# First norm of a two-layer diffusion trunk: modulation columns on TensorE in four groups, token squares summed in PSUM, first FFN pair chunk by chunk

## What is computed

```python
mod = (silu(c) @ ada_w[i] + ada_b[i])          # 9 * 1024 columns; c for latents, c_ctx for context
h   = x * rsqrt(mean(x * x) + eps) * g * (1 + mod[1]) + mod[0]
x   = x + 0.5 * mod[2] * ((silu(h @ w_gate) * (h @ w_up)) @ w_out)
```

## Time and profile before

| what | value |
|---|---|
| median of 3 runs | 2604.01 us (2602.99 to 2610.74) |
| the profiled execution | 2606.32 us, its span 2604.5 us |
| busy PE / DVE / ACT / POOL | 96% / 61% / 34% / 17% of the span |
| first 130 us, moved by DMA | 21.57 MB, 166 GB/s |
| first FFN matmul of the core | 77.26 us after the span's start |
| loop of FFN pairs (L1225) begins | 97.82 us |

### The profile page before, as it was taken

One profiled execution on the slowest core, in us unless ns is written; L12 is line 12 of the kernel. 1 busy time (PEld: TensorE's weight loads), 2 busy tenths in 40 slices (PEclk: granted clock), 3 DMA queues, 4 the chain that ended last, 5 costly groups with the idle time before them and its releaser, 6 DMA issues.

```text
span 2604.5 us, 40617 instructions
## 1 busy us (share of the span) xinstructions
PE 2510.9 (96%) x14679; PEld 2223.4 (85%) x14679; DVE 1598.4 (61%) x2500; ACT 874.5 (34%) x1358; POOL 436.7 (17%) x524
## 2 busy tenths in 40 slices
PE   6999999999799999999999999999899988999999
PEld 6888888888788888888889999998889977788887
DVE  6788667224678867883484756574777774433332
ACT  1333223122533322332242433243456553322221
POOL 2022111001212211110100000001477751000000
PEclk6899999999899999999999999999899999899999
DMA  6355543221145544542111222122110101233332
GB/s 222 109 149 157 145 126 105 64 75 39 33 133 150 168 129 129 149 145 67 44 57 57 81 59 79 50 80 65 49 49 24 48 25 57 73 100 94 93 102 87
DMA packets 363902, 238.77 MB, mean 92 GB/s; under 512 B 7633, under 2 KB 362546, under 8 KB 363826
## 3 DMA queue, kind: packets, MB, share of 16 engines
q1 hardware_dynamic: 361984, 237.01, 31.2%
q10 hardware_dynamic: 1842, 0.77, 0.1%
HBM read 235.65 MB, written 2.10 MB: 91 GB/s over the span
## 4 chain that ended last, share of the span: by engine, by line
PE 89%; DVE 5%; issue 2%; ACT 2%; POOL 1%; DMA 0%; SPq 0%; ACTq 0%; DVEq 0%; POOLq 0%
PE pu L1225 62%; PE pu L1373 11%; PE pv L1511 5%; PE pu L1233 3%; PE pu L1548 1%; DVE h_lo L2070 1%; PE pv L1539 1%; PE pu L1529 1%; DVE xn L2062 1%; POOL sqa L632 1%; PE pv L1301 1%; PE pu L1484 1%; DVE mx L2169 1%; PE pu L1635 1%; DVE a L2188 0%
## 5 line engine op out<-in xcount | busy, mean ns | idle before, releaser
L1225 PE MATMUL pu<-h_hi,w_hi 128*128 128x512 f32 x1776 | 506.9, 350 | 1.9 <-DVE w_lo L1757 1.8
L1225 PE MATMUL pu<-h_lo,w_hi 128*128 128x512 f32 x1776 | 506.2, 349 | 0.0
L1225 PE MATMUL pu<-h_hi,w_lo 128*128 128x512 f32 x1776 | 504.9, 348 | 0.0
L1757 DVE TENSOR_TENSOR w_lo<-w_raw,w_hi 128x1024 fp32r<-128x1024 f32 (+3 forms) x228 | 310.5, 1362 | 242.6 <-ACT w_hi L755 234.6
L755 ACT ACTIVATE w_hi<-w_raw 128x1024 fp32r<-128x1024 f32 (+3 forms) x228 | 247.8, 1088 | 574.1 <-PE pu L1225 510.0
L1774 DVE SCALAR_TENSOR_TENSOR ada_acc<-ada_raw,cs,ada_acc 128x384 f32<-128x384 f32 x588 | 337.3, 615 | 10.7 <-DVE ada_acc L1774 1.8
L1225 PEld LDWEIGHTS pu<-h_hi,w_hi 128*128 128x128 f32 x1776 | 284.1, 188 | 48.6 <-DVE w_lo L1757 2.2
L1225 PEld LDWEIGHTS pu<-h_hi,w_lo 128*128 128x128 f32 x1776 | 285.3, 188 | 46.3
L1225 PEld LDWEIGHTS pu<-h_lo,w_hi 128*128 128x128 f32 x1776 | 284.0, 188 | 44.1
L1985 DVE SCALAR_TENSOR_TENSOR xT<-pu,gate,xT 128x512 f32 (+3 forms) x136 | 81.3, 633 | 332.2 <-PE pu L1225 329.1
L684 POOL TENSOR_TENSOR ada_acc<-ada_acc,ada_parts 128x768 f32<-128x768 f32 x84 | 142.3, 1694 | 707.3 <-ACT ada_parts L762 667.0
(11 more groups left out here) (266 smaller groups left out, 4540.2 us busy)
## 6 DMA issues: line engine op xcount, KB each, us to landing
w_raw<-in_ffn_w_in SPq DMA_DIRECT2D x138, 512.0 KB, 3.9
ada_raw<-in_ada_w SPq DMA_DIRECT2D x84, 768.0 KB, 4.7
w_raw<-in_ffn_w_out SPq DMA_DIRECT2D x48, 704.0 KB, 4.6
w_raw<-in_ffn_w_in SPq DMA_DIRECT2D x76, 256.0 KB, 3.0
w_raw<-in_diff_w_qkv SPq DMA_DIRECT2D x24, 512.0 KB, 5.4
first_h<-in_ada_w SPq DMA_DIRECT2D x4, 1536.0 KB, 20.1
w_raw<-in_ffn_w_out SPq DMA_DIRECT2D x16, 384.0 KB, 3.5
w_raw<-in_ffn_w_out SPq DMA_DIRECT2D x16, 320.0 KB, 3.1
```

Of the source, the lines that this page charges most:

```text
L1225: last = pe.matmul(banks(ch, s_), w[:, j, :], r[:, SEG[s_]], start=(j == 0 and i == 0), stop=(j == k - 1 and i == 2))
L1757: dve.tensor_tensor(w_lo[:, ch, 0:k * P], w_raw[:, ch, 0:k * P], w_hi[:, ch, 0:k * P].bitcast(F32), ALU.subtract).then_inc(split_ready[ch], 1)
```

## The change

It rewrites the setup up to the end of the first FFN pair, in five parts.

1. All shift and scale columns are multiplied on PE. They are loaded and multiplied in four groups of two chunks of shift and two of scale (32 products each). DVE's shares and PE's sums over them are gone. The two gate chunks that were in the setup are loaded and multiplied after FFN pair 1.
2. PE sums each chunk's squares right away, with six products by the column of ones per chunk, added up in PSUM, between the transposes. POOL's additions are gone.
3. DVE runs the norm group by group, two chunks of both sections, as soon as that group's columns are there.
4. PE's first FFN pair goes chunk by chunk, with both sections and both channels for each chunk, and the column products of groups 2 and 3 stand between the chunks.
5. SP loads group 0, the first pair's weights and group 1, waits for the last transpose (groups 2 and 3 lie over the token stage), and then loads those.

```diff
-            for u in range(ADA_FIRST):
-                sp.dma_start(first_raw[u], first[:, :, u, :]).then_inc(first_in[u], 16)
+            def load_first(g):
+                for m in range(2):
+                    sp.dma_start(first_raw[:, g, :, m, :], first[:, :, m, 2 * g * P:2 * (g + 1) * P]).then_inc(first_in[g], 16)
...
+            load_first(0)
+            for ch in range(2):
+                load_unit(ch, 0, wslot(w_raw, ch, DC), ...)
+            load_first(1)
+            sp.wait_ge(xt_done, DC)
+            load_first(2)
+            load_first(3)
             load_ffn(0)
...
-            sum_chunks(0)
+            for s_ in range(2):
+                inv_rms_tokens(0, s_)
...
+            for j in range(DC):
+                act.wait_ge(x_ready, j + 1)
+                if j >= 2:
+                    act.wait_ge(x_sums, j - 1)
+                act.activation(sq[:, j % 2, :], xT[:, j, :], ACT.Square).then_inc(sq_ready, 1)
             for ch in range(2):
                 split_hi(ch, 0, DC)
-            norm_act(0)
+            for j in range(DC):
+                for s_ in range(2):
+                    norm_hi(0, s_, j)
...
+                            first_pair()
+                            for ch in range(2):
+                                unit(ch, 1, DC, lambda j: h_hi[:, j], lambda j: h_lo[:, j], n)
+                            gate_products()
+                            first = 2
...
+            def first_products(g, cols=(0, 1)):
+                pe.wait_ge(first_in[g], 32)
+                for c_ in cols:
+                    for m in range(2):
+                        at = first_at(g, m) + 2 * c_
+                        for j in range(DC):
+                            last = pe.matmul(pv[:, 2 + g % 2, at:at + 2], first_raw[:, g, j, m, c_ * P:(c_ + 1) * P],
+                                             cs[:, j::DC], start=(j == 0), stop=(j == DC - 1))
+                last.then_inc(first_done, 1)
...
+            def token_sums(j):
+                pe.wait_ge(sq_ready, j + 1)
+                own = j == DC - 1
+                for s_ in range(2):
+                    for t in range(*tiles(0, s_)):
+                        at = TT * own + t
+                        last = pe.matmul(sum_cols(s_)[:, at:at + 1], sq[:, j % 2, t * P:(t + 1) * P], ones[:, 0:1], ...)
...
+            def first_pair():
+                for ch in range(2):
+                    pe.wait_ge(split_ready[ch], 2)
+                for g in range(GROUPS):
+                    for j in (2 * g, 2 * g + 1):
+                        for s_ in range(2):
+                            pe.wait_ge(h_ready[s_], j + 1)
+                        for ch in range(2):
+                            last = chunk(ch, j, DC, h_hi[:, j], h_lo[:, j], NT)
+                            if j == DC - 1:
+                                last.then_inc(unit_done[ch], 1)
+                    if g + 2 < GROUPS:
+                        first_products(g + 2)
...
+                if j >= 2:
+                    token_sums(j - 2)
...
+            first_products(0, (0,))
+            token_sums(DC - 2)
+            token_sums(DC - 1)
+            first_products(0, (1,))
             for s_ in range(2):
                 spread(0, s_)
-            first_sums(2)
-            first_sums(3)
+            first_products(1)
             ffn_pe(0)
...
-            first_share(0)
-            first_share(1)
-            first_share(2)
             for s_ in range(2):
                 norm_rms(0, s_)
-            first_share(3)
...
+            for g in range(GROUPS):
+                first_mods(g)
+                if g == 0:
+                    for ch in range(2):
+                        split_lo(ch, 0, DC)
+                for j in (2 * g, 2 * g + 1):
+                    for s_ in range(2):
+                        norm_scale(0, s_, j)
+                for j in (2 * g, 2 * g + 1):
+                    for s_ in range(2):
+                        norm_lo(0, s_, j)
```

More of the change, by code:

```diff
@@ L548, in load_ffn @@
                     if q == 0 and ADA_COUNT[n]:
-                        for f in range(2):
+                        for f in range(int(n == 0), 2):
                             in_pair(0, f, False)
                         sp.wait_ge(h_ready[1], DC * (2 * n + 1))
+                        if n == 0:
+                            sp.dma_start(gate_raw[:], first[:, :, 2, 0:GATE_CH * P]).then_inc(gate_in, 16)
                         load_granule(n, 0)
@@ new lines, in gate_products @@
+            def gate_products():
+                pe.wait_ge(gate_in, 16)
+                for c_ in range(GATE_CH):
+                    at = 2 * (GATE_FIRST + c_)
+                    for j in range(DC):
+                        pe.matmul(pv[:, 2, at:at + 2], gate_raw[:, j, c_ * P:(c_ + 1) * P], cs[:, j::DC],
+                                  start=(j == 0), stop=(j == DC - 1))
+            def token_sums(j):
[4 more added lines that the diff above has]
+                        at = TT * own + t
+                        last = pe.matmul(sum_cols(s_)[:, at:at + 1], sq[:, j % 2, t * P:(t + 1) * P], ones[:, 0:1],
+                                         start=(j == 0 and t == tiles(0, s_)[0] or own), stop=(j >= DC - 2), skip_group_check=True)
+                    if own:
+                        last.then_inc(var_done, 1)
+                if not own:
+                    last.then_inc(x_sums, 1)
@@ L2066, in norm_seg @@
                     if j + 1 < DC:
[L2067 to L2071, removed]
+                        norm_scale(i, s_, j + 1)
+                    norm_lo(i, s_, j)
                     if j in at:
@@ L2073, in norm_seg, with first_mods @@
                         at[j]()
+            def first_mods(g):
+                dve.wait_ge(first_done, g + 2)
+                for m in range(2):
+                    c0, at = DC * m + 2 * g, first_at(g, m)
+                    last = dve.tensor_tensor(mod[:, :, c0:c0 + 2], pv[:, 2 + g % 2, at:at + 4].rearrange("p (c s) -> p s c", s=2),
+                                             par[:, 0:1, c0:c0 + 2].broadcast_to((P, 2, 2)), ALU.add)
+                last.then_inc(first_mod, 1)
+                dve.wait_ge(first_mod, 2 * g + 1)
+                c0 = C_NORM_G + 2 * g
+                dve.scalar_tensor_tensor(amul[:, 0, :, 2 * g:2 * g + 2], mod[:, :, DC + 2 * g:DC + 2 * g + 2], 1.0,
+                                         par[:, 0:1, c0:c0 + 2].broadcast_to((P, 2, 2)), ALU.add, ALU.mult).then_inc(first_mod, 1)
+                dve.wait_ge(first_mod, 2 * g + 2)
```

131 lines of the change are left out of this document (49 added, 82 removed).

## The result

| | before | changed |
|---|---|---|
| median | 2604.86 us (4 runs, 2602.99 to 2610.74) | 2630.11 us (4 runs, 2627.85 to 2634.44) |
| ratio | | 1.0092, 95% interval 1.008 to 1.0105 |
| span of the profiled execution | 2604.5 us | 2626.1 us |
| pair 1 (the FFN pair behind the first) begins | 97.82 us | 113.47 us |

A forecast was written before the change was run, and what follows sets the result against it. PE was taken as the bound, with small products at the low clock: first pair ending 16.2 us later, 1.3 us wait and 3.5 us gate make 21.0 us, so 2625 us against the 2604.0 median; range 2615 to 2636.

The forecast's parts named there:

- The clock stays low in the setup: Setup on PE: small products hold PE at 1.2 GHz, so the first FFN matmul comes near 73 us.
- The sign that was named: Setup: PEclk 0.50 from the first products to the first FFN matmuls, with PE busy all the time.
- Transposes and sums: PE from 13.70 us: 36 transposes 7.2 us, 48 token sums 21.1 us, all at the low clock.
- Products: Shift and scale products of groups 0 and 1 on PE: 64 at 0.433 us, 27.7 us.
- The first pair: First FFN pair with groups 2 and 3's products between its chunks: 40.65 us, ending at 114.0 us.
- The 5.0 of the forecast: Products of groups 2 and 3 inside the first pair: 5.0 us at the high clock before it falls.
- Behind the pair: After the first FFN pair: 1.3 us new wait for w_hi and w_lo, 3.5 us for 16 gate products.
- DVE and the loads inside the pair priced at nothing: First FFN pair: DVE's norm work and the later loads of groups 2 and 3 never hold PE, no cost.
- the 21.0 forecast: Whole kernel: 16.2 us later pair end, 1.3 us wait and 3.5 us gate products, 21.0 us slower.
- Full clock: Setup and first pair: gapless PE stays at 2.4 GHz from 17 us; 16.7 us gained, 2587 us; chance 0.08.
- No rise between the groups: First pair: clock low through groups 0 and 1 and both product groups; 34 us lost, 2638 us; chance 0.06.
- Early rise: Setup: transposes lift the clock near 17 us and it holds meanwhile; 9 us lost, 2613 us; chance 0.10.

The follow-up runs named there:

- experiment 5: Changed kernel with each shift and scale product's moving operand 16 columns wide instead of 2: 2625.7 us, 1.0065 of the kernel before.
- experiment 2: Changed kernel with each shift and scale product's moving operand 128 columns wide instead of 2: 2604.2 us, 0.9989 of the kernel before.
- experiment 8: Changed kernel, squares on POOL, 128-column products, plus last group of the first pair by channels and w_lo made earlier: 2593.2 us, 0.9939 of the kernel before.
- experiment 10: Changed kernel with only 2 of the 16 gate products: one execution, 2618.8 us; loop begins 17.57 us behind pair 1's start, against 20.69.
- experiment 1: Changed kernel with squares added up on POOL again and 12 token sums on PE instead of 48: 2619.6 us, 1.0046 of the kernel before.
- experiment 7: Kernel before with only the squares summed on PE between the transposes and POOL's additions gone: 2612.6 us, 1.0019 of the kernel before.
- experiment 4: Changed kernel with the products of groups 2 and 3 moved ahead of an unbroken first FFN pair: 2630.0 us, against the changed kernel's 2630.1.
- experiment 3: Changed kernel with squares summed on POOL and shift and scale products 128 columns wide: 2590.8 us, 0.9941 of the kernel before.
- experiment 6: Changed kernel with 128-column shift and scale products, run once more for a second profile: 2604.2 us, 11.7 more than the first profiled execution.

## Why the prediction was right

- *The clock stays low in the setup.* Shown, by durations. The sign that was named, PEclk 0.50 up to the first FFN matmuls, did not print: the changed kernel's profile prints 1.00 there, while its products take 0.42 us; the same products read 0.50 in experiment 5, where an earlier change is on record. The term had the largest share of the forecast, and experiments 2 and 5 separate it from everything else in that edit.
- *Transposes and sums, 28.3 us and the last transpose near 34.* The transposes ended at 33.87, and from 13.70 on transposes and sums took 27.6 us together.
- *Products.* 0.433 was taken, 0.42 measured (6.62 + 6.83 + 13.44 for 64, 26.9 instead of 27.7); the first FFN matmul came at 71.4 instead of 73.3.
- *The first pair.* FFN groups 5.7, 6.5 and, to channel 0's end, 8.9 us, against 6.15, 6.15 and 10.35 to channel 1's, which ended at 112.0, 9.9 us after the group's start; products 9.6 and 8.7 against 9.0 twice. The whole pair took 40.5 us (40.65). The clock fell about 4 and 5 us into the products of groups 2 and 3 (at 81.3 and 98.4). The 5.0 of the forecast had been chosen between 3.6 us and never, without a reason for it; that this came so close is in part luck.
- *Behind the pair.* A wait of 1.45 us for w_lo (1.3), 3.47 us for the gate (3.5). Experiments 8 and 10 show both.
- *DVE and the loads inside the pair priced at nothing.* Right: PE has no gap there.
- *What was too small.* The path by the gate gives 15.65 + 3.47 = 19.1 us, 1.9 less than the 21.0 forecast; the spans differ by 21.6 and the medians by 25.3 (the interval is about 21 to 27). The 2.5 us between path and spans lie in later stages that the change doesn't touch: the same ACT and DVE instructions come 19 us later than before up to 650 us, 20 from 700 to 1800 and 21.5 from 2200 on, and near these places PEclk changes a few times in every execution. The rest is between executions: the profiled one of the kernel before lay 1.5 us over its median, that of the changed kernel 2.3 under. So the sum was 1.9 too long on its own path and lacked 6 us of the difference of the medians, for which it had no term. What the forecast had as one number against one median has a scatter of some us on both sides. Whether the change adds to that scatter stays open.
- *The parts.* Everything but part 2 costs 13 us by the medians (experiment 1), part 2 alone 6.5 (experiment 7), together 19.5 of the 25; parts 1, 3, 4 and 5 were not taken apart further, save that the products inside the pair are not the loss (experiment 4).
- *The rivals.* "Full clock" is what experiment 3 built, but for 22 to 29 us: it took the edit to make the products wide, and gave 14 to 16 us, near the 17 of that rival's sum. "No rise between the groups" didn't come. "Early rise" came for 3.4 us at most, in three of the seven profiled executions that begin so. The rule that a PE kept busy continuously gets its full clock, from the Trainium skill's "TensorE: Matmul & The Clock Gate" (the table of why this matters for kernels), would have forecast that rival's 2587. PEclk 0.50 with PE busy 13.00 of 13.00 us (experiment 5) contradicts it for thin products.

## What to carry to other kernels

Before you pack small products onto TensorE, price them at the clock they will leave behind, not at the one at which you saw them: streams of products with 1, 2 or 16 moving columns ran at half clock here, but for their first 2 to 5 us where the clock was up ahead of them, and the first FFN matmuls behind them ran at half clock too. If such products can't be avoided, widen the moving operand with a broadcast (it cost next to nothing at the high clock, 0.223 us against 0.22), or leave the additions to an engine that is idle. And an engine that comes earlier meets loads that nobody waited for before: look up when they land.

## What the runs showed that I had not expected

- A product of 128 fp32 columns costs about as much as one of 2 at the high clock: 32 in 7.14 us, 0.223 each, against 0.217 for the 16 of the gate (3.47 us). At the low one it is alike too: 25 records in 5.00 us from 33 to 38 us in experiment 6, 0.40 a product. The 32 records of half the first group took 4.59 and 6.19 us in the two profiles of one kernel, by how soon the clock rose.
- PEclk prints 1.00 for the stretch ahead of its first change: up to 17 us in the kernel before, 74.5 in the changed one, 103 in experiment 4. The weight loads (0.20 us each, then 0.107) and the products' 0.42 us show that the clock was low there; the first windows of a profile have to be read by durations.
